# One-hots of the expert gate maps, token by token: pointer-scalar instructions in place of broadcast compares and products

## The chip, the cores and the metric

One Trainium2 chip, one of its cores. The metric is the device time of one execution in microseconds, median over runs of the same program.

## The reference, cut to what matters

Two transformer blocks over 256 tokens of width 1024 in f32. The first has a short convolution mixer, an attention mixer and two gated MLPs; the second a hybrid mixer and, last, the PEER feed-forward, where the change lies:

```python
def peer_ffn(x, w_q, sub_keys, u_tab, v_tab):      # 128 x 128 experts, 8 heads, 16 of them a head and token
...
    cand_idx = top_i[..., 0, :, None] * PEER_NKEYS + top_i[..., 1, None, :]
    best_s, pos = lax.top_k(cand, K)
    eidx = jnp.take_along_axis(cand_idx, pos, axis=-1)
    gate = jax.nn.softmax(best_s, axis=-1)
    hpre = jnp.einsum("nd,nhkd->nhk", xc, u_tab[eidx])
    act = gate * jax.nn.gelu(hpre, approximate=False)
    return jnp.einsum("nhk,nhkd->nd", act, v_tab[eidx])
```

Each token has 8 x 16 = 128 chosen experts. An expert has two keys, a (first sub-key) and b (second sub-key), each 0 to 127.

## The kernel before, in words

**Weights.** All weight matrices come as 546 chunks of 128 x 1024 f32 through a ring of three (`RING`), loaded by DMAs on SP's queue (L370). Each chunk is split in two fp32r halves: ACT writes the high half (`split_hi`, L383), then DVE and POOL write the rest, `raw - hi` (`split_lo`, L397), DVE the columns up to `cut` and POOL those behind it; in the expert stage the cut is 384, so DVE does 384 columns and POOL 640. TensorE multiplies a chunk with three products per 128 columns (L428, L429, L430), 24 matmuls a chunk. When it is done, ACT and then DVE and POOL take the chunk three places on.

**Expert stage.** The kernel gathers nothing. It goes through all 128 x 128 experts: 128 chunks upward (`UP0`, one for each key a, all keys b on the partitions) and 128 chunks downward (`DOWN0`). The gelu of the upward results lies in `emap` [b, a, token]. It is multiplied by a map of gates [b, a] for each token, which is zero where the token has not chosen the expert. A token's map is a matrix product over its 128 choices (on the partitions): `hot_b` (choice x 128, one where b is the choice's second key) times `hot_a` (choice x 64, the choice's gate where a is its first key). The gate is split in three bf16 parts so that bf16 matmuls keep its precision; hence three `hot_a` and three matmuls a token (L1495). 64 of the keys a make a half; eight tokens (`GT`) make a batch, 32 batches (`NB`) a half.

**The loops around the change.** `peer_dve` is DVE's program of the stage. In `second` (half 0, beside the second half of the upward chunks), a batch is: `hots`, two `walk_dve` (L397, 384 columns), `take_gates` of the batch before (L1485, `emap` times the map in PSUM). In `third` (half 1, beside the first half of the downward chunks) it is: `z_rest` (L1591, the low half of the gated experts), `hots`, `walk_dve`, `z_rest`, `walk_dve`, `take_gates`. `fourth` does the last 64 downward chunks and has no one-hots. TensorE's batch is two chunks (48 matmuls of 256 columns) and then `gates_of_batch_pe` (24 matmuls of 64 columns), which waits for `hot_ready`. `hots` in turn waits for `gm_done`, the gate matmuls of the batch before, as there is one set of `hot_a` and `hot_b`. Each engine runs its own instructions in the order written; there is no planner.

`hots` itself, for eight tokens at once: L1470 compares an iota with the first key, both inputs broadcast, into `hot_a[:, 2]` (512 columns); L1472 does the same for the second key into `hot_b` (1024 columns); then DVE waits for L1470's result (`dc.need`), and L1476 multiplies it with the three gate parts, the last in place, behind one more wait (`dc.link`).

`steps` writes the first rounds (up to `first`) and the last as straight code and the rest as a loop on the engine, six batches a turn here; in a loop, addresses and semaphore values that depend on the round are computed in registers by the engine's queue.

Of the kernel before, what the change touches and what calls it, by code (L numbers as in the profile page):

```python
# [16 lines left out]
ALU = mybir.AluOpType  # L17
# [3 lines left out]
P = 128  # L21
# [74 lines left out]
def steps(eng, chain, lo, hi, body, fn, first=0, per=0):  # L96

    n = lo
    while n < min(first, hi):
        fn(Step(n))  # L100
        n += 1
    turns = (hi - n) // body
    if turns > 1:
        with eng.Fori(0, turns) as i:
            if chain is not None:
                at = chain.n
                chain.i, chain.per = i, per * body
            for u in range(body):
                fn(Step(n + u, body, i))
            if chain is not None:  # L110
                assert chain.n - at == per * body, (chain.n - at, per, body)
                chain.n = at + per * body * turns
                chain.i = None
        n += body * turns
    while n < hi:
        fn(Step(n))
        n += 1
# [16 lines left out]
HALF = NKEY // 2  # L134
GT = 8


def build(nc, stream, xT, par, con, alibi_t, wg, wcmpk, wcmpv, peT, subk, y):
# [141 lines left out]
    idx = b_.take(2, T, dt=BF16)  # L280
    gate_left = b_.take(1, T)
    gate_part = b_.take(3, T, dt=BF16)
    iota_b = b_.take(P, dt=BF16)
    hot_b, hot_a = b_.take(GT, P, dt=BF16), b_.take(3, GT, HALF, dt=BF16)
# [120 lines left out]
    def walk_dve(dve, st, a, b):  # L405
        split_lo(dve, nc.vector, st, a, b + RING)
# [5 lines left out]
    def range_dve(dve, lo, hi):  # L412
        steps(dve, None, lo, hi, RING, lambda st: walk_dve(dve, st, 1, 0))
# [331 lines left out]
    def prev(st, n=1):  # L745
        return Step(st.s - n, st.stride, st.i)
# [714 lines left out]

    NB = T // GT

    def hots(dve, dc, half, st):
        if half or st.s >= 1:
            dve.wait_ge(gm_done, st.lin(1, NB * half))
        tok = bass.ds(st.lin(GT), GT)
        sa, sb_ = [P, GT, HALF], [P, GT, P]
        iota = iota_b
        dc.mark(nc.vector.tensor_tensor(hot_a[:, 2], iota[:, half * HALF:half * HALF + HALF].unsqueeze(1).broadcast_to(sa),  # L1470
                                        idx[:, 0, tok].unsqueeze(2).broadcast_to(sa), ALU.is_equal))
        nc.vector.tensor_tensor(hot_b, iota.unsqueeze(1).broadcast_to(sb_),  # L1472
                                idx[:, 1, tok].unsqueeze(2).broadcast_to(sb_), ALU.is_equal)
        dc.need()
        for i in range(3):
            ins = nc.vector.tensor_tensor(hot_a[:, i], hot_a[:, 2],  # L1476
                                          gate_part[:, i, tok].unsqueeze(2).broadcast_to(sa), ALU.mult)
            if i == 1:
                dc.link(ins)
        ins.then_inc(hot_ready, 1)  # L1480

    def take_gates(dve, half, st):
        dve.wait_ge(gm_done, st.lin(1, NB * half + 1))
        v = emap_of(half, st)
        nc.vector.tensor_tensor(v, v, ps[:, 6 + st.mod(2), :].rearrange("p (t a) -> p t a", t=GT), ALU.mult)\  # L1485
            .then_inc(gm_taken, 1)
# [75 lines left out]
    def peer_dve(dve, dc):  # L1562

        done, us = 0, 0.0
        for price in peer_top(dve, dc):
            us += price
            while done < HALF and us >= 1.8 * (done + 1):
                walk_dve(dve, Step(done), 1, UP0)
                done += 1
        range_dve(dve, UP0 + done, UP0 + HALF)  # L1570
        dve.wait_ge(tk_act, 10)
        dc.link(nc.vector.tensor_tensor(gate_left[:, 0], ps[:, 2, 0:T], gate_part[:, 0], ALU.subtract))
        dc.link(nc.vector.tensor_copy(gate_part[:, 1], gate_left[:, 0]))
        dc.link(nc.vector.tensor_tensor(gate_part[:, 2], gate_left[:, 0], gate_part[:, 1], ALU.subtract))

        def second(st):
            hots(dve, dc, 0, st)
            for u in range(2):
                walk_dve(dve, st, 2, UP0 + HALF + u - 1) if st.s or u else None
            if st.s >= 1:  # L1580
                take_gates(dve, 0, prev(st))

        steps(dve, dc, 0, NB, 6, second, first=1, per=2)
        walk_dve(dve, Step(NKEY - 1), 1, UP0)
        take_gates(dve, 0, Step(NB - 1))

        def z_rest(st, a, b):

            p = st.mod(2, a, b)
            dve.wait_ge(ez_hi, st.lin(a, b + 1))  # L1590
            nc.vector.tensor_tensor(ez[p][1], emap[:, st.lin(a, b), :], ez[p][0].bitcast(F32), ALU.subtract)\  # L1591
                .then_inc(z_ready, 1)

        z_rest(Step(0), 1, 0)

        def third(st, last=False):
            z_rest(st, 2, 1)
            hots(dve, dc, 1, st)
            if st.s >= 1:
                walk_dve(dve, st, 2, DOWN0 - 1)  # L1600
            if not last:
                z_rest(st, 2, 2)
            walk_dve(dve, st, 2, DOWN0)
            if st.s >= 1:
                take_gates(dve, 1, prev(st))

        steps(dve, dc, 0, NB - 1, 6, third, first=1, per=2)
        third(Step(NB - 1), last=True)
        take_gates(dve, 1, Step(NB - 1))

        def fourth(st):
            z_rest(st, 1, 0)
            walk_dve(dve, st, 1, DOWN0 - 1)

        steps(dve, None, HALF, NKEY - RING, 6, fourth)
        for n in range(NKEY - RING, NKEY):
            fourth(Step(n))
        dve.wait_ge(chunk_done, NCH)
# [4 lines left out]
    with nc.Block() as block:  # L1623
# [110 lines left out]
        def _(dve):  # L1734
# [35 lines left out]
            range_dve(dve, CH["pq"], UP0 - RING)  # L1770
            range_dve(dve, UP0 - RING, UP0)
            peer_dve(dve, dc)
            residual_dve(dve, dc)
            norm_dve(dve, dc, 7, "fin2")
# [147 lines left out]
```

## Time and profile before

| | us |
|---|---|
| median of three runs | 2238.18 |
| lowest and highest of them | 2234.65 and 2238.45 |
| profiled execution, first to last instruction | 2237.8 |
| busy in it: PE, DVE, ACT, POOL | 1986.2, 1614.8, 875.4, 884.5 |

The times of instructions below are of the one profiled execution; the profile gives its span (2237.8 us) and no other time of its own. PE is TensorE, DVE VectorE, ACT ScalarE, POOL GpSimd. "L1476" is line 1476 of the kernel; a line can be a helper's, as L397, which both DVE and POOL run. A row of the timeline has the start, the time taken, the engine, line, operation, what is written and read (m is SBUF, ps is PSUM), shapes and a count; in brackets the idle time before it and what ended that. Rows of one line that follow each other are merged into one with their count. Neighbours on DVE overlap in it by some 0.08 us, so prices are read from start to start where that can be done.

### The profile page before, as it was taken

How to read it: one execution, taken by the hardware profiler on the slowest of the kernel's cores; microseconds unless marked ns; L12 is line 12 of the kernel's file. 1: busy time of each engine (PE TensorE's matmuls, PEld its weight loads, DVE VectorE, ACT ScalarE, POOL GpSimd, SP SyncE). 2: the span in 40 equal slices, each digit the busy share in tenths (PEclk: the TensorE clock that was granted, in tenths of full speed). 3: DMA queues.
4: the chain of work that ended last, by engine and by line, in shares of the span. 5: the costliest groups of instructions: out<-in, count | busy, mean ns of one | idle time of the engine just before them, and what ended most of it. 6: DMA issues, size and time to landing. Idle time of an engine off the chain costs nothing.

```text
span 2237.8 us, 44421 instructions
## 1 busy us (share of the span) xinstructions
PE 1986.2 (89%) x15848; PEld 1919.1 (86%) x15848; DVE 1614.8 (72%) x2502; ACT 875.4 (39%) x1317; POOL 884.5 (40%) x584
## 2 busy tenths in 40 slices
PE   7979988998999699797898999898897888879897
PEld 7979988887999699787797999898887888878887
DVE  5568877545888423545655499779999999996665
ACT  4333433433434353633443455533333222324443
POOL 3524442303444153101254355654444333335553
PEclk9989998858999798657998999999999888889999
DMA  5535553404555153100264355543433333334443
GB/s 197 182 98 188 177 175 104 132 0 151 178 187 178 57 183 119 48 1 1 93 202 157 113 177 163 166 142 132 139 142 113 115 120 120 114 117 154 153 159 103
DMA packets 80278, 293.72 MB, mean 131 GB/s; under 512 B 8960, under 2 KB 9120, under 8 KB 79824
## 3 DMA queue, kind: packets, MB, share of 16 engines
q1 hardware_dynamic: 79632, 289.96, 38.9%
q0 software_dynamic: 576, 2.79, 0.3%
q8 instruction: 48, 0.79, 0.1%
q14 instruction: 22, 0.18, 0.0%
HBM read 291.67 MB, written 1.05 MB: 131 GB/s over the span
## 4 chain that ended last, share of the span: by engine, by line
PE 62%; DVE 23%; issue 9%; ACT 4%; DVEq 1%; DMA 0%; ACTq 0%; POOL 0%; SPq 0%; POOLq 0%
PE ps L428 17%; PE ps L430 16%; PE ps L429 16%; DVE m L1476 5%; DVE m L397 4%; DVE m L1591 3%; PE ps L434 3%; DVE m L1485 2%; PE ps L469 2%; DVE m L1470 2%; ACT m L383 1%; PE ps L759 1%; PE ps L758 1%; DVE m L521 1%; PE ps L1495 1%
## 5 line engine op out<-in xcount | busy, mean ns | idle before, releaser
L428 PE MATMUL ps<-m,m 128*128 128x256 f32 x4336 | 1270.9, 293 | 124.0 <-DVE m L1591 48.7
L397 POOL TENSOR_TENSOR m<-m,m 128x352 fp32r<-128x352 f32 (+1 forms) x546 | 867.4, 1590 | 1148.3 <-ACT m L383 1148.0
L429 PE MATMUL ps<-m,m 128*128 128x256 f32 x4336 | 1253.6, 289 | 0.0
L430 PE MATMUL ps<-m,m 128*128 128x256 f32 x4336 | 1251.3, 289 | 0.0
L428 PEld LDWEIGHTS ps<-m,m 128*128 128x128 f32 x4336 | 859.1, 198 | 140.0 <-issue 70.2
L429 PEld LDWEIGHTS ps<-m,m 128*128 128x128 f32 x4336 | 859.8, 198 | 0.6 <-issue 0.2
L430 PEld LDWEIGHTS ps<-m,m 128*128 128x128 f32 x4336 | 859.2, 198 | 0.0
L397 DVE TENSOR_TENSOR m<-m,m 128x672 fp32r<-128x672 f32 (+1 forms) x546 | 531.5, 985 | 407.2 <-ACT m L383 406.0
L383 ACT ACTIVATE m<-m 128x1024 fp32r<-128x1024 f32 x546 | 575.7, 1055 | 604.4 <-PE ps L430 586.1
L1476 DVE TENSOR_TENSOR m<-m,m 128x512 bf16<-128x512 bf16 x192 | 172.4, 923 | 9.6 <-DVE m L1476 1.5
L1591 DVE TENSOR_TENSOR m<-m,m 128x256 fp32r<-128x256 f32 x128 | 167.9, 1313 | 9.8 <-ACT m L1551 9.6
L1533 ACT ACTIVATE m<-ps 128x256 f32 (+1 forms) x128 | 49.2, 384 | 231.2 <-PE ps L430 231.1
L434 PEld LDWEIGHTS ps<-m,m 128*128 128x128 f32 (+1 forms) x412 | 75.5, 268 | 32.9 <-issue 16.6
L1495 PE MATMUL ps<-m,m 128*128 128x64 bf16 x1536 | 56.2, 194 | 47.5 <-DVE m L1476 47.5
L434 PE MATMUL ps<-m,m 128*128 128x128 f32 (+1 forms) x412 | 87.8, 380 | 11.5 <-ACT m L884 9.7
L1495 PEld LDWEIGHTS ps<-m,m 128*128 128x128 bf16 x1536 | 48.6, 98 | 55.4 <-DVE m L1476 37.5
L1485 DVE TENSOR_TENSOR m<-m,ps 128x512 f32 (+1 forms) x64 | 84.6, 1323 | 0.0
L1472 DVE TENSOR_TENSOR m<-m,m 128x1024 bf16<-128x1024 bf16 x64 | 77.6, 1212 | 0.0
L469 PE MATMUL ps<-m,m 128*128 128x256 f32 x128 | 45.1, 529 | 32.1 <-ACT m L500 32.1
L469 PEld LDWEIGHTS ps<-m,m 128*128 128x128 f32 x128 | 34.5, 277 | 41.2 <-ACT m L500 27.3
L594 ACT ACTIVATE m<-m 128x256 f32<-128x256 f32 x44 | 18.4, 418 | 126.5 <-DVE m L556 126.5
L813 ACT ACTIVATE m<-m,m 128x128 f32<-128x128 f32 x64 | 28.6, 447 | 84.5 <-PE ps L434 76.3
(200 smaller groups left out, 1292.4 us busy)
## 6 DMA issues: line engine op xcount, KB each, us to landing
m<-stream SPq DMA_DIRECT2D x546, 512.0 KB, 3.4
m<-alibi_t POOLq DMA_DIRECT2D x1, 1536.0 KB, 8.6
m<-con SPq DMA_DIRECT2D x1, 1353.0 KB, 10.2
m<-xT SPq DMA_DIRECT2D x1, 1024.0 KB, 4.9
y<-m SPq DMA_DIRECT2D x4, 256.0 KB, 2.4
m<-wcmpk POOLq DMA_DIRECT2D x1, 512.0 KB, 5.1
m<-wcmpv POOLq DMA_DIRECT2D x1, 512.0 KB, 5.7
m<-par SPq DMA_DIRECT2D x1, 178.0 KB, 5.3
```

What stands on the lines that cost most here:

```text
L383: nc.scalar.activation(w_hi[:, r, :], raw[:, r, :], ACT.Copy).then_inc(hi_done, 1)
L397: ops.tensor_tensor(w_lo[:, r, cols], raw[:, r, cols], w_hi[:, r, cols].bitcast(F32), ALU.subtract)\
L428: nc.tensor.matmul(out, lhs[0], rhs[0], start=start, stop=False, **kw)
L429: nc.tensor.matmul(out, lhs[0], rhs[1], start=False, stop=False, **kw)
L430: return nc.tensor.matmul(out, lhs[1], rhs[0], start=False, stop=stop, **kw)
L434: return nc.tensor.matmul(out, v, unit, start=True, stop=True)
L469: ins = nc.tensor.matmul(ps[:, 7, 0:T], ones[:, 0:P], sq[:, j, :], start=(j == 0), stop=(j == 7))
L1472: nc.vector.tensor_tensor(hot_b, iota.unsqueeze(1).broadcast_to(sb_), idx[:, 1, tok].unsqueeze(2).broadcast_to(sb_), ALU.is_equal)
L1476: ins = nc.vector.tensor_tensor(hot_a[:, i], hot_a[:, 2], gate_part[:, i, tok].unsqueeze(2).broadcast_to(sa), ALU.mult)
L1485: nc.vector.tensor_tensor(v, v, ps[:, 6 + st.mod(2), :].rearrange("p (t a) -> p t a", t=GT), ALU.mult)\
L1495: ins = nc.tensor.matmul(out, hot_b[:, q, :], hot_a[:, i, q, :], start=i == 0, stop=i == 2)
L1591: nc.vector.tensor_tensor(ez[p][1], emap[:, st.lin(a, b), :], ez[p][0].bitcast(F32), ALU.subtract)\
```

## The change

`hots` no longer works on eight tokens at once. For each of the eight tokens of a batch it issues four `tensor_scalar` instructions. The first compares the iota (128 columns) with the token's second key, a pointer scalar (one value a partition), and writes the token's part of `hot_b`. Three more compare 64 columns of the iota with the first key and multiply by one of the three gate parts, both pointer scalars, and write the token's part of `hot_a[:, i]`. No product reads a compare's result any more, so both waits of DVE on itself go, and with them the chain object `dc`. The two loops of batches on DVE become straight code (`first=NB`). TensorE's program and the semaphores between engines stay.

```diff
-    def hots(dve, dc, half, st):
+    def hots(dve, half, st):
         if half or st.s >= 1:
             dve.wait_ge(gm_done, st.lin(1, NB * half))
-        tok = bass.ds(st.lin(GT), GT)
-        sa, sb_ = [P, GT, HALF], [P, GT, P]
-        iota = iota_b
-        dc.mark(nc.vector.tensor_tensor(hot_a[:, 2], iota[:, half * HALF:half * HALF + HALF].unsqueeze(1).broadcast_to(sa),
-                                        idx[:, 0, tok].unsqueeze(2).broadcast_to(sa), ALU.is_equal))
-        nc.vector.tensor_tensor(hot_b, iota.unsqueeze(1).broadcast_to(sb_),
-                                idx[:, 1, tok].unsqueeze(2).broadcast_to(sb_), ALU.is_equal)
-        dc.need()
-        for i in range(3):
-            ins = nc.vector.tensor_tensor(hot_a[:, i], hot_a[:, 2],
-                                          gate_part[:, i, tok].unsqueeze(2).broadcast_to(sa), ALU.mult)
-            if i == 1:
-                dc.link(ins)
+        for q in range(GT):
+            one_tok = bass.ds(st.lin(GT, q), 1)
+            nc.vector.tensor_scalar(hot_b[:, q, :], iota_b, idx[:, 1, one_tok], None, ALU.is_equal)
+            for i in range(3):
+                ins = nc.vector.tensor_scalar(hot_a[:, i, q, :], iota_b[:, half * HALF:half * HALF + HALF],
+                                              idx[:, 0, one_tok], gate_part[:, i, one_tok],
+                                              ALU.is_equal, ALU.mult)
         ins.then_inc(hot_ready, 1)
...
-        steps(dve, dc, 0, NB, 6, second, first=1, per=2)
+        steps(dve, None, 0, NB, 6, second, first=NB)
...
-        steps(dve, dc, 0, NB - 1, 6, third, first=1, per=2)
+        steps(dve, None, 0, NB - 1, 6, third, first=NB)
```

(The two calls `hots(dve, dc, ...)` lose `dc` as well.)

## Rows read from the trace of the kernel before

**Rows 1.** The page: busy time by engine, and the group of L1476.
```profile
PE 1986.2 (89%) x15848; PEld 1919.1 (86%) x15848; DVE 1614.8 (72%) x2502; ACT 875.4 (39%) x1317; POOL 884.5 (40%) x584
...
L1476 DVE TENSOR_TENSOR m<-m,m 128x512 bf16<-128x512 bf16 x192 | 172.4, 923 | 9.6 <-DVE m L1476 1.5
```

**Rows 2.** Busy time by stretches: `second`, then `third`.
```profile
core 0: us, PE busy (x) PEld busy (x) DVE busy (x) ACT busy (x) POOL busy (x), PEclk, DMA share, GB/s
1469.00:1712.00 243.00, 214.52 (x2278) 208.82 (x2276) 235.95 (x253) 86.01 (x128) 112.85 (x64) 0.98 0.39 134
1712.00:2005.00 293.00, 241.56 (x2280) 235.98 (x2280) 279.43 (x319) 86.45 (x127) 111.55 (x63) 0.87 0.34 115
```

**Rows 3.** L1472 in each stretch: ns min/median/max, first and last start (us).
```profile
L1472 DVE TENSOR_TENSOR m<-m,m x32: 1207/1212/1226, 1469.1 to 1705.5; 128x1024 bf16<-128x1024 bf16 x32
...
L1472 DVE TENSOR_TENSOR m<-m,m x32: 1205/1212/1218, 1716.9 to 2000.9; 128x1024 bf16<-128x1024 bf16 x32
```

**Rows 4.** TensorE's timeline in `second`, and its waits there (us, times, longest).
```profile
1566.96 0.87 PE L1495 MATMUL ps<-m,m 128*128 128x64 bf16 x24 [0.89 <-DVE m L1476]
1567.87 0.28 PE L429 MATMUL ps<-m,m 128*128 128x256 f32 x1
...
1568.70 0.28 PE L430 MATMUL ps<-m,m 128*128 128x256 f32 x1
...
PE ps L1495 <- DVE m L1476: 19.2, 17, 2.1
```

**Rows 5.** DVE's timeline over one batch of `second`.
```profile
1581.81 1.01 DVE L397 TENSOR_TENSOR m<-m,m 128x384 fp32r<-128x384 f32 x2
1582.75 1.35 DVE L1485 TENSOR_TENSOR m<-m,ps 128x512 f32 x1
1584.02 0.80 DVE L1470 TENSOR_TENSOR m<-m,m 128x512 bf16<-128x512 bf16 x1
...
1587.91 2.39 DVE L397 TENSOR_TENSOR m<-m,m 128x384 fp32r<-128x384 f32 x2
```

**Rows 6.** POOL's timeline over the same batch.
```profile
1582.44 1.82 POOL L397 TENSOR_TENSOR m<-m,m 128x640 fp32r<-128x640 f32 x1 [1.10 <-ACT m L383]
1587.38 2.02 POOL L397 TENSOR_TENSOR m<-m,m 128x640 fp32r<-128x640 f32 x1 [3.11 <-ACT m L383]
```

**Rows 7.** L1591 over the span: ns min/median/max, first and last start.
```profile
L1591 DVE TENSOR_TENSOR m<-m,m x128: 403/1741/1799, 1715.6 to 2217.8; 128x256 fp32r<-128x256 f32 x128
```

**Rows 8.** The timeline near 1384 us, DVE and POOL: scalar instructions without pointer.
```profile
1383.87 0.30 DVE L1424 TENSOR_SCALAR m<-m 128x256 uint32<-128x256 uint32 x1
1384.08 1.66 DVE L1425 TENSOR_SCALAR m<-m 128x256 uint32<-128x256 uint32 x1
...
1383.94 1.65 POOL L397 TENSOR_TENSOR m<-m,m 128x640 fp32r<-128x640 f32 x1 [1.00 <-ACT m L383]
```

**Rows 9.** Two lines over the span: with a pointer scalar, and without.
```profile
L521 DVE SCALAR_TENSOR_TENSOR m<-m,m,m x64: 476/478/487, 15.4 to 2234.6; 128x256 f32<-128x256 f32 x64
...
L726 DVE TENSOR_TENSOR m<-m,m x16: 418/426/426, 358.6 to 408.1; 128x256 f32<-128x256 f32 x16
```

**Rows 10.** DVE's timeline at 446 us: 64 columns from PSUM, pointer scalar in SBUF.
```profile
446.53 0.28 DVE L944 TENSOR_SCALAR m<-ps,m 128x64 f32 x1 [0.16 <-DVE m L841]
446.73 0.28 DVE L945 TENSOR_SCALAR m<-ps,m 128x64 f32 x1
```

**Rows 11.** DVE's timeline at 1301 us: two instructions that start closest together.
```profile
1301.77 0.07 DVE L1401 MATCH_VALUE_LOAD m<-m,m 128x8 f32 x1
1301.83 0.28 DVE L1401 FIND_INDEX8 m<-m,m 128x8 uint32<-128x128 f32 x1
```

**Rows 12.** The timeline at 32 us, POOL and DVE: `tensor_scalar` from SBUF with pointer.
```profile
31.59 1.63 POOL L397 TENSOR_TENSOR m<-m,m 128x352 fp32r<-128x352 f32 x1 [1.26 <-ACT m L383]
...
32.77 0.59 DVE L553 TENSOR_SCALAR m<-m,m 128x256 f32<-128x256 f32 x1
```

**Rows 13.** Busy time by stretches, straight code of many small DVE instructions.
```profile
1280.00:1340.00 60.00, 58.14 (x485) 57.93 (x484) 58.91 (x244) 30.76 (x44) 33.94 (x20) 1.00 0.52 175
```

More of the change, by code:

```diff
@@ L1576, in second @@
         def second(st):
-            hots(dve, dc, 0, st)
+            hots(dve, 0, st)
             for u in range(2):
@@ L1597, in third @@
             z_rest(st, 2, 1)
-            hots(dve, dc, 1, st)
+            hots(dve, 1, st)
             if st.s >= 1:
```

## The prediction

> **What bounds the kernel now.** I read the page first: VectorE (DVE) is busy for 72% of the span and TensorE for 89%, so over the whole span TensorE looks like the limit, and the products of L1476 are the largest DVE group that the change touches [rows 1]. A mean over stages says little, so I cut the span with the view of busy time by stretches. From 1469 to 1712 us (up half of the expert stage: `second`, 32 batches of eight tokens) DVE is busy for 236 of 243 us, and from 1712 to 2005 us (`third`, 32 batches) for 279 of 293 us [rows 2]. Here DVE is the bound. The first and last starts of L1472, which runs once a batch, give the pace: (1705.5 - 1469.1) / 31 = 7.63 us a batch in `second`, (2000.9 - 1716.9) / 31 = 9.16 us in `third` [rows 3]. TensorE needs less: the 24 gate matmuls take up to 0.87 us, and the chunk matmuls come every (1568.70 - 1567.87) / 7 = 0.119 us, 48 a batch, 5.7 us, so some 6.5 us a batch at the full clock; it waits for L1476 [rows 4].
>
> The DVE timeline shows how a batch is spent [rows 5]. The one-hots (L1470, L1472, three of L1476) run from 1584.02 to 1587.91: **3.89 us**, nothing in their way. The two L397 at 1581.81 take 0.94 us, L1485 1.27 us. So a free batch is 3.89 + 0.94 + 1.27 = 6.10 us, and 7.63 - 6.10 = **1.53 us** is something else. The timeline of POOL names it [rows 6]: its subtraction starts at 1587.38 and ends at 1589.40, and the DVE pair of L397 that starts at 1587.91 takes 2.39 instead of 1.01 us. A DVE instruction on two SBUF inputs stands still until POOL's ends. POOL's other one, at 1582.44, lies mostly beside L1485, which reads PSUM, and costs little. POOL runs two a batch, some 1.6 us each without its own waiting: 3.2 us, of which DVE loses 1.53. In `third` two L1591 come on top, 0.40 us each when free [rows 7], less the 0.08 by which neighbours overlap in this view: free 6.10 + 0.64 = 6.74 us, the other 2.42 us blocked or idle.
>
> **The change, part by part.** Removed, a batch: five instructions of 0.6 to 1.2 us and two waits on DVE's own results, together the 3.89 us. Added: 32 `tensor_scalar`, eight with 128 columns and one pointer scalar, 24 with 64 columns and two. The loops become straight code; that drops register work which DVE's queue does beside running instructions, so I count it as nothing. No DMA, matmul or semaphore between engines moves: `hot_ready` still comes after the last write, so TensorE cannot start on the first token early.
>
> What does one cost? The trace has no such form in bf16 with two pointers, so I build it up. *Streaming.* L1472 (1024 columns, median 1212 ns [rows 3]) against L726 (256 columns, 426 ns [rows 9]) gives (1212 - 426) / 768 = 1.02 ns a column, one a cycle. L1424, a `tensor_scalar` from SBUF to SBUF without pointer [rows 8], does 256 columns in 0.30 us, 0.13 less than L726: two columns a cycle. I take that rate: 0.067 us for 128 columns, 0.033 for 64. *Fixed part.* L1424 starts 0.21 us before the next, less 0.13 of streaming is 0.08. A pointer is not free: L521 takes 478 ns where L726, the same columns without one, takes 426, so 0.052 us more [rows 9]: 0.13. A second way: L944 and L945, 64 columns with one pointer, start 0.20 us apart [rows 10]; 0.065 of it is streaming at one a cycle, 0.135 is fixed. They agree; I take **0.13 us**. *Second pointer.* No row; nothing to 0.055 us; I take nothing, as both come from the same place in one instruction. So 0.197 us for hot_b and 0.163 for each hot_a: a token 0.197 + 3 x 0.163 = 0.686, a batch 8 x 0.686 = **5.5 us** against 3.89. The break-even price is 3.89 / 32 = 0.122 us an instruction, and the columns hardly matter: the fixed part alone exceeds it.
>
> Bounds of the price: below, the closest starts on DVE, 0.06 us (MATCH_VALUE_LOAD, then the next) [rows 11], plus streaming: 8 x (0.127 + 3 x 0.093) = 3.25 us. Above, a full second pointer and one column a cycle: 8 x (0.263 + 3 x 0.252) = 8.2 us; with the second pointer but two columns a cycle 8 x (0.197 + 3 x 0.218) = 6.8 us.
>
> The Trainium skill (VectorE: DVE Perf Modes, the perf-mode tier table) lets a bf16 `tensor_scalar` from SBUF to SBUF stream four elements a cycle, and `tensor_tensor` two. By that the new ones would cost 4.8 us a batch in place of 5.5, and the time would be some 43 us below my forecast. No row here shows four a cycle; and L1472, a `tensor_tensor` broadcast along its columns, runs at one, not two [rows 3].
>
> *Blocking.* One might hope that one-source instructions escape POOL. They don't: L1425 starts at 1384.08 behind POOL's start at 1383.94 and takes 1.66 us where L1424 took 0.30 [rows 8], and L553, a `tensor_scalar` from SBUF with a pointer, takes 0.59 us, ending at 33.36, 0.14 us behind POOL's end at 33.22 [rows 12]. The Trainium skill (SBUF — State Buffer, SBUF: two separate sides) says the same of this port pair and gives it to whoever starts first for the whole instruction; by that rule, the trace agrees. With a longer stretch of blockable work, fewer POOL instructions fall beside L1485. In `second` I raise the loss from 1.53 to 2.1 us (`third`, whose batches are as long as the new ones, loses 2.42 with its idle time; 3.2 is the most); in `third` I leave 2.42.
>
> **Sum.** `second`: 0.94 + 1.27 + 5.5 + 2.1 = 9.8 us, +2.2 a batch, x 32 = +70. `third`: 6.74 - 3.89 + 5.5 + 2.42 = 10.8, +1.6, x 32 = +52. All else: 0, for no other stage runs this code, and ACT, POOL and the stream only follow TensorE. Together +122 us. The profiled execution spans 2237.8 us, 0.4 below the median of the three runs, 2238.18; forecast **2360 us**. Late next is TensorE: it would idle 3.3 us or more a batch in both stages. In `third`, where it idles now, the granted clock is 0.87 [rows 2]; I expect 0.75 to 0.9 in both. Even if half a batch's work ran at 1.2 GHz, its 6.5 us would be 9.8, no more than DVE's pace; if all did, 13.0 us, it would set it.
>
> **Rivals.**
> *Faster.* The pointer is fetched beside the instruction before, and short instructions follow each other at the 0.06 us of MATCH_VALUE_LOAD plus streaming: 3.25 us a batch, 0.64 less, x 64 = -41: 2197 us. It decides from 0.122 us an instruction downwards. For it: nothing in the trace shows short bf16 streams otherwise; against it: L944 at 64 columns still pays the whole fixed part [rows 10]. The Trainium skill (VectorE: DVE Perf Modes, The TRN2 errata) gives 58 cycles plus the columns by the mode's factor, 77 and 94 ns here, 2.6 us a batch; that would be some -80 us, TensorE's 6.5 us then being the floor in `second`. The same section warns that many small tiles pay the fixed cost each time. Chance 0.10 for either.
> *Second pointer priced like the first.* 6.8 us a batch, 1.3 more, x 64 = +85: 2445 us. Chance 0.18.
> *Clock.* TensorE idles so long that it stays at 1.2 GHz: 13.0 us a batch, against 9.8 and 10.8: 3.2 and 2.2 more, x 32 = +173 on the forecast: about 2530. Against it: 0.87 in `third` is a mix of the two levels, mostly 2.4 GHz, and at the low level TensorE would be busy all the time. Chance 0.03.
> *The straight code starves DVE.* Some 2,500 more instructions must be fetched. Against it: 244 DVE instructions in 60 us, straight code, kept it busy for 58.9 [rows 13]; the new pace is lower. Chance 0.02, and it only adds.
> *No difference*: the price happens to be 0.12 us. Chance 0.03; 2238.
> The forecast itself, price 0.14 to 0.19 us and a loss of 1.5 to 2.8 us a batch: 0.64.
>
> **How the numbers follow.** The range goes from the cheap end of the forecast (a fixed part of 0.11 us, so 4.9 us a batch, and a loss of 1.6 and 2.0: 8.7 and 9.8 us a batch, about 2290) to the second pointer with its spread (2450); outside lie the faster rival, the clock and a bit of each edge, 2 in 10. About 0.2% (4.5 us) is what a measurement of this kernel can tell from no change. Faster 0.11, within 0.03, slower 0.86.
>
> **What would show it.** In the profile after: the new instructions start 0.15 to 0.17 us (64 columns) and about 0.2 us (128) apart when POOL is idle; some of them last 1.6 to 1.8 us while POOL works; batches 9 to 11 us apart; TensorE's wait before the gate matmuls at 3 us a batch; the last stage unchanged at 220 us. It is wrong if the starts are under 0.12 us apart, or if the new ones run on while POOL works.

## The result, and the profile after

The changed kernel takes **2398.99 us** (2397.09 to 2401.06) against 2237.82 us for the kernel before, measured beside it: ratio 1.0727, 95% interval 1.0711 to 1.0742, slower by 161 us. The forecast was 2360 us, slower by 122, range 2290 to 2450.

Busy time by stretches of the kernel after, cut where `second` and `third` begin and end (columns as in [rows 2]):

```profile
core 0: us, PE busy (x) PEld busy (x) DVE busy (x) ACT busy (x) POOL busy (x), PEclk, DMA share, GB/s
1469.00:1805.00 336.00, 240.59 (x2281) 234.04 (x2279) 334.42 (x1121) 86.11 (x130) 108.32 (x64) 0.88 0.29 101
1805.00:2165.00 360.00, 256.82 (x2296) 250.42 (x2297) 359.11 (x1180) 85.64 (x125) 108.21 (x63) 0.82 0.25 90
2165.00:2397.00 232.00, 199.82 (x1564) 191.24 (x1561) 151.65 (x143) 89.42 (x132) 120.08 (x62) 0.97 0.42 143
```

Nearly everything lost lies in two stretches. `second` is 336 us long where it was 247 (to the first one-hot of `third`), `third` some 360 where it was 292: 157 of the 159 us by which the two profiled executions differ. The stage begins at 1468.5 us in the trace before and at 1468.7 in this one. DVE is busy for 334 of 336 and for 359 of 360 us: it was the bound and is so more than before. From the first one-hot instruction of the first batch to that of the last, over 31, a batch takes 10.43 us in `second` (7.63 before) and 11.34 us in `third` (9.16 before, same reading as [rows 3]).

The two new lines over the span, where L1470, L1472 and L1476 were: L1469 writes hot_b, L1471 writes hot_a (ns min/median/max, first and last start):

```profile
L1469 DVE TENSOR_SCALAR m<-m,m x512: 233/243/1647, 1468.7 to 2163.5; 128x128 bf16<-128x128 bf16 x171
...
L1471 DVE TENSOR_SCALAR m<-m,m,m x1536: 282/290/1712, 1468.9 to 2164.0; 128x64 bf16<-128x64 bf16 x192
```

The *smaller* instruction lasts longer, 290 ns for 64 columns against 243 for 128. It is the one with two pointers. DVE's timeline within a batch of `second` gives the starts:

```profile
1533.11 0.25 DVE L1469 TENSOR_SCALAR m<-m,m 128x128 bf16<-128x128 bf16 x1
1533.28 0.71 DVE L1471 TENSOR_SCALAR m<-m,m,m 128x64 bf16<-128x64 bf16 x3
1533.90 0.25 DVE L1469 TENSOR_SCALAR m<-m,m 128x128 bf16<-128x128 bf16 x1
1534.06 1.98 DVE L1471 TENSOR_SCALAR m<-m,m,m 128x64 bf16<-128x64 bf16 x3
1535.95 0.24 DVE L1469 TENSOR_SCALAR m<-m,m 128x128 bf16<-128x128 bf16 x1
1536.11 0.70 DVE L1471 TENSOR_SCALAR m<-m,m,m 128x64 bf16<-128x64 bf16 x3
1536.73 0.24 DVE L1469 TENSOR_SCALAR m<-m,m 128x128 bf16<-128x128 bf16 x1
1536.90 1.99 DVE L1471 TENSOR_SCALAR m<-m,m,m 128x64 bf16<-128x64 bf16 x3
```

and POOL's beside it, where [rows 6] stood:

```profile
1534.43 1.57 POOL L397 TENSOR_TENSOR m<-m,m 128x640 fp32r<-128x640 f32 x1 [3.47 <-ACT m L383]
1536.88 1.55 POOL L397 TENSOR_TENSOR m<-m,m 128x640 fp32r<-128x640 f32 x1 [0.89 <-ACT m L383]
```

A free token takes 1533.90 - 1533.11 = 0.79 us, a batch eight times that, 6.3 us. By the medians of start to start over all of them it is 0.163 us for hot_b and 0.206 for each hot_a, 0.781 a token, **6.25 us** a batch against 3.89. And two groups of three that should take 0.7 us take 2.0: each has one instruction that stands still through one of POOL's two, and ends 0.04 us behind it. TensorE waits for the one-hots before each batch's gate matmuls (L1489, L1495 in the kernel before), 194.4 us in all, 3.0 a batch:

```profile
PE ps L1489 <- DVE m L1471: 194.4, 62, 5.9
```

### The profile page after: what moved, and what is told of

It reads as the page before. It is cut to its first block, busy times and chain, and to the rows that moved or that the text cites. A ratio compares the mean times of both kernels' runs of the same rounds, so it can differ in the third digit from the quotient of the medians.

```text
span 2397.2 us, 45347 instructions
## 1 busy us (share of the span) xinstructions
PE 2029.8 (85%) x15848; PEld 1959.7 (82%) x15848; DVE 1790.2 (75%) x4230; ACT 874.4 (36%) x1317; POOL 876.2 (37%) x584
## 4 chain that ended last, share of the span: by engine, by line
PE 55%; DVE 38%; ACT 3%; issue 3%; DMA 0%; DVEq 0%; POOL 0%; SPq 0%; ACTq 0%; POOLq 0%
DVE m L1471 17%; PE ps L428 15%; PE ps L429 15%; PE ps L430 15%; DVE m L1469 5%; DVE m L397 3%; DVE m L1585 3%; DVE m L1479 3%; PE ps L434 3%; PE ps L469 2%; PE ps L759 1%; ACT m L383 1%; PE ps L758 1%; DVE m L521 1%; PE ps L777 1%
## 5 line engine op out<-in xcount | busy, mean ns | idle before, releaser
L397 POOL TENSOR_TENSOR m<-m,m 128x352 fp32r<-128x352 f32 (+1 forms) x546 | 859.2, 1575 | 1316.0 <-ACT m L383 1315.8
L428 PEld LDWEIGHTS ps<-m,m 128*128 128x128 f32 x4336 | 872.1, 201 | 107.4 <-issue 63.4
L429 PEld LDWEIGHTS ps<-m,m 128*128 128x128 f32 x4336 | 871.2, 201 | 0.6 <-issue 0.2
L430 PEld LDWEIGHTS ps<-m,m 128*128 128x128 f32 x4336 | 868.5, 200 | 0.0
L397 DVE TENSOR_TENSOR m<-m,m 128x672 fp32r<-128x672 f32 (+1 forms) x546 | 485.4, 900 | 408.1 <-ACT m L383 406.9
L1471 DVE TENSOR_SCALAR m<-m,m,m 128x64 bf16<-128x64 bf16 x1536 | 460.5, 356 | 0.0
L1489 PE MATMUL ps<-m,m 128*128 128x64 bf16 x1536 | 75.7, 219 | 194.4 <-DVE m L1471 194.4
L1489 PEld LDWEIGHTS ps<-m,m 128*128 128x128 bf16 x1536 | 66.8, 115 | 206.8 <-DVE m L1471 140.7
L1469 DVE TENSOR_SCALAR m<-m,m 128x128 bf16<-128x128 bf16 x512 | 157.5, 308 | 1.1 <-PE ps L1489 1.1
L1585 DVE TENSOR_TENSOR m<-m,m 128x256 fp32r<-128x256 f32 x128 | 141.1, 1104 | 2.0 <-ACT m L1545 2.0
L1479 DVE TENSOR_TENSOR m<-m,ps 128x512 f32<-128x512 f32 x64 | 82.7, 1294 | 0.0
L469 PEld LDWEIGHTS ps<-m,m 128*128 128x128 f32 x128 | 34.7, 278 | 41.2 <-ACT m L500 27.4
```

Source lines behind the costliest of these rows:

```text
L397: ops.tensor_tensor(w_lo[:, r, cols], raw[:, r, cols], w_hi[:, r, cols].bitcast(F32), ALU.subtract)\
L428: nc.tensor.matmul(out, lhs[0], rhs[0], start=start, stop=False, **kw)
L429: nc.tensor.matmul(out, lhs[0], rhs[1], start=False, stop=False, **kw)
L430: return nc.tensor.matmul(out, lhs[1], rhs[0], start=False, stop=stop, **kw)
L469: ins = nc.tensor.matmul(ps[:, 7, 0:T], ones[:, 0:P], sq[:, j, :], start=(j == 0), stop=(j == 7))
L1469: nc.vector.tensor_scalar(hot_b[:, q, :], iota_b, idx[:, 1, one_tok], None, ALU.is_equal)
```

## The experiments

Each was timed beside the kernel before. Line numbers shift with the edits, so the gate matmul is L1488, L1489, L1495, L1497 or L1498 in what follows. First, those that take the change apart.

**The straight code alone.** The kernel before with `first=NB` in both calls of `steps`:

```diff
-        steps(dve, dc, 0, NB, 6, second, first=1, per=2)
+        steps(dve, dc, 0, NB, 6, second, first=NB, per=2)
...
-        steps(dve, dc, 0, NB - 1, 6, third, first=1, per=2)
+        steps(dve, dc, 0, NB - 1, 6, third, first=NB, per=2)
```

> The kernel before with its two DVE loops of batches written as straight code, nothing else. My theory (the price of the small instructions makes the loss): no difference, 2238 us within 5, batches 7.6 and 9.2 us apart. Rival (straight code itself costs, through fetching or through the order of waits): at least a quarter of the 161 us, so 2278 us or more.

Measured: 2233.18 us, ratio 0.9984 (0.9973 to 0.9996), batches 7.53 and 9.15 us apart. The straight code costs nothing; it may give 4 us.

**The loops kept.** The other way round: the changed kernel with `first=1`.

```diff
-        steps(dve, None, 0, NB, 6, second, first=NB)
+        steps(dve, None, 0, NB, 6, second, first=1)
```

(and the same for `third`)

> The changed kernel with its two DVE loops of batches kept as loops (as in the kernel before), so that the addresses of keys and gates are computed by DVE's queue. In the kernel before, such register work comes 0.11 to 0.13 us apart in the queue. Queue theory: a 64-column instruction needs two of them, more than the 0.206 us that it takes itself, so starts 0.22 to 0.26 us apart, hots 7 us or more a batch, time 2440 us or more. Rival (the queue works ahead and hides it): 2399 us.

Measured: 2397.56 us, ratio 1.0732 (1.0708 to 1.0756), as the changed kernel; batches 10.43 and 11.34 us, starts 0.163 and 0.206 us. My theory of the queue was wrong and the rival right. The queue's rows for the line show why:

```profile
L1471 DVEq FUSED_REGOPS  x960: 57/67/82, 1480.0 to 2150.6; - x192
L1471 DVEq ALU_OP  x480: 40/40/40, 1480.1 to 2150.4; - x160
```

That is 1440 for the 1440 instructions in the loops (60 batches of 24): one each, not two. Where the queue works ahead (at 1480 us), a token's four, hot_b's among them, take 0.54 us from start to start, and the engine needs 0.781 us a token; so they run beside the instructions before them.

**One pointer less.** The product with the gate left out of hot_a (the result then lacks the gates):

```diff
-                                              idx[:, 0, one_tok], gate_part[:, i, one_tok],
-                                              ALU.is_equal, ALU.mult)
+                                              idx[:, 0, one_tok], None, ALU.is_equal)
```

> The changed kernel with hot_a written by a compare with one pointer scalar alone: the product with the gate is left out. In the changed kernel the 64-column instructions start 0.206 us apart, the 128-column ones 0.163. Pointer theory (every pointer scalar costs 0.05 to 0.06 us): 64 columns with one pointer start 0.15 us apart, hots take 8 x (0.163 + 3 x 0.15) = 4.9 us in place of 6.25, time 2399 - 64 x 1.35 = about 2313 us. Rival (a second pointer is free, 0.2 us is the least for 64 columns): starts stay at 0.2 us, time 2399 us.

**No pointer at all.** Constants in their places, both operations of hot_a kept (keys and gates are left out):

```diff
-            nc.vector.tensor_scalar(hot_b[:, q, :], iota_b, idx[:, 1, one_tok], None, ALU.is_equal)
+            nc.vector.tensor_scalar(hot_b[:, q, :], iota_b, 3.0, None, ALU.is_equal)
...
-                                              idx[:, 0, one_tok], gate_part[:, i, one_tok],
-                                              ALU.is_equal, ALU.mult)
+                                              3.0, 1.0, ALU.is_equal, ALU.mult)
```

> The changed kernel with constants in place of all pointer scalars; hot_a keeps its two operations, the keys and gates are left out of the one-hots. Pointer theory: fixed part 0.08 us, so 0.11 us for 128 columns and 0.095 for 64, hots 3.2 us a batch, batches some 6.9 and 8.2 us apart, time about 2190 us, below the kernel before. Rival (the second operation costs, not the second pointer): 64 columns still start 0.04 us further apart than 128 columns do, hots 4 us or more, time 2240 us or more.

Measured: 2304.09 us (ratio 1.0302, 1.0271 to 1.0334) and 2157.46 us (0.9653, 0.9631 to 0.9674). Hot_a with one pointer, hot_a with none, and hot_b with none:

```profile
L1471 DVE TENSOR_SCALAR m<-m,m x1536: 222/229/1631, 1468.1 to 2067.0; 128x64 bf16<-128x64 bf16 x192
```

```profile
L1471 DVE TENSOR_SCALAR m<-m x1536: 161/169/1591, 1470.5 to 1923.2; 128x64 bf16<-128x64 bf16 x192
...
L1469 DVE TENSOR_SCALAR m<-m x512: 175/182/1595, 1470.4 to 1923.0; 128x128 bf16<-128x128 bf16 x171
```

A ladder: 169, 229, 290 ns for none, one, two pointers. From start to start (medians): 0.086, 0.146, 0.206 us. **Each pointer costs 0.060 us, the second as much as the first.** e2_one_pointer takes the product away together with the pointer, so it can't tell the two apart; hot_b can. It has one operation, 128 columns, and starts 0.163 us before the next with its pointer and 0.102 without: 0.061 for a pointer alone. Take that off e2_one_pointer's 0.146 and 64 columns with one operation and no pointer would be 0.085, with two operations they measure 0.086: the second operation costs nothing. Between 128 and 64 columns lie 0.016 us (0.102 and 0.086; 0.163 and 0.146 with a pointer), 0.25 ns a column, a quarter of the 1.02 ns that the prediction found for one column a cycle: four a cycle. So the price is 0.069 + 0.060 a pointer + 0.00026 a column. Without pointers the small instructions beat the broadcast form: the changed form was lost on its scalars, not on its number. The whole times say less than the starts do, since something else ends a batch as the one-hots get shorter: batches of e3_no_pointer are 6.71 us apart in `second`, 0.2 above TensorE's 6.5, and it came out 33 us below the 2190 expected.

**Only hot_b by token.** e1_straight with the one line:

```diff
-        nc.vector.tensor_tensor(hot_b, iota.unsqueeze(1).broadcast_to(sb_),
-                                idx[:, 1, tok].unsqueeze(2).broadcast_to(sb_), ALU.is_equal)
+        for q in range(GT):
+            one_tok = bass.ds(st.lin(GT, q), 1)
+            nc.vector.tensor_scalar(hot_b[:, q, :], iota, idx[:, 1, one_tok], None, ALU.is_equal)
```

> The kernel before in straight code, with hot_b alone written by eight pointer-scalar compares a batch; hot_a stays with its broadcast compare and three products. Theory of the price by instruction: 8 x 0.163 = 1.30 us in place of 1.135, 0.17 a batch, 64 batches: 11 us over e1_straight (2233), so 2244. The other 150 us of the loss belong to the 24 hot_a instructions. Rival (splitting into small instructions itself disturbs the stage, whatever its sum): 2260 us or more.

Measured: 2238.62 us, ratio 1.0010 (0.9995 to 1.0024), 5 us over e1_straight, where 11 were expected. Little or nothing of the 161 us is hot_b's; the hot_a instructions, 24 of the 32, have it. The compares for hot_b start 0.163 us apart here too.

**POOL out of the way.** The split's border in the expert stage moved, in the changed kernel and in the kernel before:

```diff
-CUT, CUT_PEER = 672, 384
+CUT, CUT_PEER = 672, 1016
```

> The changed kernel with the split of the expert stage's chunks nearly all on DVE: 1016 columns, POOL has 8. DVE's L397 grows by 0.66 us a chunk, 1.3 a batch. Lock theory (POOL's instruction holds the one-source DVE instructions up, 1.7 us a batch in second and 1.9 in third): no one-hot instruction lasts over 0.5 us, batches 8.46 + 1.3 = 9.8 us in second (10.16 now) and 9.1 + 1.3 = 10.4 in third (11.0 now); the first half of the upward chunks, where DVE picks the top 16, gets slower. Rival (the long instructions have another cause): long ones stay, batches 11.5 and 12.3 us.

> The kernel before, its one-hots untouched, with 1016 of the 1024 columns of the expert chunks' split on DVE and 8 on POOL (the same edit as in e4_pool_out). Lock theory: free batches of 6.1 + 1.3 = 7.4 us in second (7.6 now) and 6.7 + 1.3 = 8.0 in third (9.2 now), and the last stage 20 us shorter as in e4_pool_out, so 2238 - 7 - 37 - 20 = about 2174 us. Rival (in the kernel before POOL's help is worth its waits, since broadcast tensor_tensor hides them): 2238 us or slower.

Measured: 2322.57 us (1.0388, 1.0371 to 1.0405), batches 9.67 and 10.37 us; and 2168.23 us (0.9691, 0.9676 to 0.9706), batches 7.22 and 8.00 us. The one-hots in the first, with POOL left 8 columns:

```profile
L1471 DVE TENSOR_SCALAR m<-m,m,m x1536: 282/290/346, 1469.0 to 2109.2; 128x64 bf16<-128x64 bf16 x192
...
L1469 DVE TENSOR_SCALAR m<-m,m x512: 232/243/287, 1468.8 to 2108.6; 128x128 bf16<-128x128 bf16 x171
```

The longest is 346 ns, where it was 1712. DVE does 2.6 times the columns of the split and both kernels gain, 76 and 69 us: POOL's help cost DVE more in waits than it took off. The gain isn't all in the stretches of the change. In e5_pool_out_before `second` is 13 us shorter and `third` 36, and what comes after the last one-hots 22; in e4_pool_out it is 24, 30 and 22. (The stage itself begins between 1463.8 and 1471.0 us in these profiles, whatever was changed in it, so a few us of a profiled execution are not the edit's.) Of what I expected, one part failed: the upward half before `second` did not get slower (`second` starts at 1468.8 us in e4_pool_out). In the second kernel L397 takes 1208 ns for 1016 columns, L1476 lasts 690 ns in the mean, not 923, and L1591 lasts 424 in the median, not 1741 [rows 7]:

```profile
L397 DVE TENSOR_TENSOR m<-m,m 128x1016 fp32r<-128x1016 f32 x128 | 152.0, 1208 | 0.4 <-ACT m L383 0.4
L1476 DVE TENSOR_TENSOR m<-m,m 128x512 bf16<-128x512 bf16 x192 | 127.0, 690 | 9.6 <-DVE m L1476 1.5
...
L1591 DVE TENSOR_TENSOR m<-m,m x128: 401/424/453, 1697.7 to 2142.3; 128x256 fp32r<-128x256 f32 x128
```

**A better way to the same aim.** The broadcast form runs at one column a cycle [rows 3]. If that comes from the inputs that repeat along the innermost dimension, a layout with tokens innermost would double it: the key and the gate then have step one, and the iota is stored repeated, once. The price: TensorE reads its one-hots with a step. First with all eight tokens innermost, a step of 16 bytes, for hot_a, then for hot_b too:

```diff
...
+    iota_t = nc.alloc_sbuf_tensor_at("iota_t", [P, P * GT], BF16, offset=base + 4 * (A0 + NKEY * T))[:, :]\
+        .rearrange("p (k t) -> p k t", k=P)
...
-        dc.mark(nc.vector.tensor_tensor(hot_a[:, 2], iota[:, half * HALF:half * HALF + HALF].unsqueeze(1).broadcast_to(sa),
-                                        idx[:, 0, tok].unsqueeze(2).broadcast_to(sa), ALU.is_equal))
+        dc.mark(nc.vector.tensor_tensor(hot_a[:, 2], iota_t[:, half * HALF:half * HALF + HALF, :],
+                                        idx[:, 0, tok].unsqueeze(1).broadcast_to(sa), ALU.is_equal))
...
-                ins = nc.tensor.matmul(out, hot_b[:, q, :], hot_a[:, i, q, :], start=i == 0, stop=i == 2)
+                ins = nc.tensor.matmul(out, hot_b[:, q, :], hot_a[:, i, :, q], start=i == 0, stop=i == 2)
```

> The kernel before with hot_a laid out with the token innermost, so that no tensor_tensor input is broadcast along its innermost dimension (an iota repeated eight times is made once, 0.5 us per partition row); TensorE then reads its 64 moving columns with a step of eight. Theory (the broadcast along the columns keeps these tensor_tensor at one column a cycle, and with the token innermost they run at two): L1470 and L1476 take 0.34 us in place of 0.60, hots 1.07 us less a batch; second comes near TensorE's floor of 6.5 us, time about 2238 - 32 x 0.9 - 32 x 1.0 = 2175 us. Rival (they stay at one a cycle, or the stepped reads slow the gate matmuls by as much): 2238 us or more.

> As e7_token_inner_a, with hot_b token innermost too, so that the stationary operand is read with a step of eight. Theory: another 0.53 us a batch off DVE; second is at TensorE's floor, third gains: about 2155 us. Rival (the stepped weight load is slow: 24 of them a batch, 0.1 us each now, so a doubling gives 2.4 us a batch back): 2230 us or more.

Measured: 2257.68 us (1.0099, 1.0085 to 1.0114) and 2320.60 us (1.0383, 1.0362 to 1.0403): the rivals' side. DVE did as the theory said, and TensorE paid. The compare, the gate matmul and its load in e7_token_inner_a:

```profile
L1471 DVE TENSOR_TENSOR m<-iota_t,m x64: 409/426/451, 1471.0 to 2022.0; 128x512 bf16<-128x512 bf16 x64
...
L1497 PEld LDWEIGHTS ps<-m,m x1536: 95/117/128, 1475.1 to 2029.9; 128*128 128x128 bf16 x192
L1497 PE MATMUL ps<-m,m x1536: 273/294/296, 1475.1 to 2030.0; 128*128 128x64 bf16 x192
```

The compare takes 426 ns where L1470 took about 682 when free; the one-hots take 2.7 us when free. But the gate matmul takes 294 ns where it took 193, and from start to start it is 0.116 us where it was 0.029. Batches of `second` are 8.51 us apart with 5.7 of chunks in them, and DVE now waits for the gate matmuls (L1497, 77.9 us). With the stationary operand stepped too, a batch takes 9.65 us. Of these 1.14 us more, only some 0.15 is the stepped operand itself: the gate matmuls start 0.122 us apart, 24 of them. So the time is on the rival's side, but not by the 2.4 us a batch of slower loads that it stood for. The rest is the clock in the chunk matmuls, granted at 0.88 in `second` where e7_token_inner_a had 0.99, though TensorE was busy for 307 of 310 us:

```profile
1469.00:1779.00 310.00, 307.36 (x2271) 305.54 (x2269) 142.40 (x255) 84.57 (x128) 112.51 (x64) 0.88 0.33 108
...
1600.20 0.28 PE L431 MATMUL ps<-m,m 128*128 128x256 f32 x1
...
1601.10 0.41 PE L430 MATMUL ps<-m,m 128*128 128x256 f32 x1
1601.31 0.41 PE L431 MATMUL ps<-m,m 128*128 128x256 f32 x1
```

In 23 of the 32 batches the clock is at its lower level (1.2 GHz) for some 3.4 us, and the chunk matmuls then come 0.213 us apart in place of 0.119; over the 48 of a batch that is 1.0 us in the mean. It falls 0.3 to 0.7 us behind the last of the gate matmuls. What makes it fall there and not in e7_token_inner_a is not shown.

Then in pairs of tokens, [pair, column, 2], a step of 4 bytes, alone and with the border of the split moved to 1016 and to 704:

```diff
...
+        sa, sb_ = [P, GT // 2, HALF, 2], [P, GT // 2, P, 2]
+
+        def of_pair(v, shape):
+            return v.rearrange("p (g t) -> p g t", t=2).unsqueeze(2).broadcast_to(shape)
+
+        dc.mark(nc.vector.tensor_tensor(hot_a[:, 2], iota_t[:, half * HALF:half * HALF + HALF, :].unsqueeze(1).broadcast_to(sa),
+                                        of_pair(idx[:, 0, tok], sa), ALU.is_equal))
+        nc.vector.tensor_tensor(hot_b, iota_t.unsqueeze(1).broadcast_to(sb_), of_pair(idx[:, 1, tok], sb_), ALU.is_equal)
...
+                ins = nc.tensor.matmul(out, hot_b[:, q // 2, :, q % 2], hot_a[:, i, q // 2, :, q % 2], start=i == 0, stop=i == 2)
```

> The kernel before with the one-hots laid out in pairs of tokens (pair, column, token of the pair): no tensor_tensor input is broadcast along its innermost dimension, and TensorE reads with a step of two bf16 (4 bytes) in place of the 16 of e7 and e8. Theory (two columns a cycle need only an innermost pair, and a step of 4 bytes is free for TensorE where 16 was not): hots 2.1 us a batch in place of 3.66, second at TensorE's floor of 6.5 to 6.7 us, third 7.5, so 2238 - 32 - 52 = about 2155 us. Rival (any step slows the gate matmuls): 2200 us or more.

> e12_pairs with 1016 of the split's columns on DVE and 8 on POOL. DVE in second 2.1 + 2.3 + 1.3 = 5.7 us a batch and 6.4 in third, without waits for POOL: both stages at TensorE's 6.5 to 6.7 us, and the last stage 20 us shorter as in e5: 2238 - 32 - 80 - 20 = about 2106 us. Rival (POOL's share is worth more once DVE has slack): 2155 us or more.

> e12_pairs with 704 columns on DVE and 320 on POOL, between the two: POOL's instruction is half as long (0.8 us in place of 1.6), so DVE waits less for each. Lock theory: a time between e12 and e13, about 2125 us. Rival (any instruction of POOL costs about as much as a long one): no better than e12.

Measured: 2132.77 us (0.9549, 0.9529 to 0.9569), **2099.08 us** (0.9391, 0.9370 to 0.9411) and 2106.09 us (0.9422, 0.9402 to 0.9442). The order is the one forecast for the lock, not the sizes: 2155, 2106 and 2125 us were expected, so the pairs alone gave 22 us more than that, and e14_pairs_cut704 lies close to e13_pairs_pool_out, not halfway. The last two are 7 us apart with intervals that overlap. The gate matmuls in e12_pairs are as short as in the kernel before, and so is the compare on DVE as in e7:

```profile
L1475 DVE TENSOR_TENSOR m<-iota_t,m x64: 408/422/429, 1468.0 to 1891.8; 128x512 bf16<-128x512 bf16 x64
...
L1498 PEld LDWEIGHTS ps<-m,m x1536: 96/97/103, 1470.9 to 1896.0; 128*128 128x128 bf16 x192
L1498 PE MATMUL ps<-m,m x1536: 191/193/205, 1470.9 to 1896.0; 128*128 128x64 bf16 x192
```

In e13_pairs_pool_out both stretches have changed their bound:

```profile
1469.00:1681.00 212.00, 208.36 (x2287) 206.85 (x2285) 180.91 (x259) 86.03 (x130) 65.92 (x64) 1.00 0.46 159
1681.00:1892.00 211.00, 210.11 (x2304) 208.73 (x2304) 200.64 (x319) 86.04 (x126) 19.57 (x63) 0.99 0.46 156
```

TensorE is busy for 208 of 212 and 210 of 211 us, at the full clock; the batches are 6.50 and 6.60 us apart, which is the 6.5 us that the prediction worked out as its floor [rows 4]. The pairs alone had brought `second` there already, and `third` nearly (e12_pairs: 6.49 and 6.85 us). Of the 34 us that POOL's columns add, the profiles have 8 in `third` and 23 in the last stage. This kernel beats the kernel before by some 136 us and the changed one by 300.

## Why the prediction was right, and which term was mis-sized

The time fell inside the range, and the direction, the bound and the waits for POOL were right. The price of an instruction, on which all rests, was wrong twice, in opposite directions; that the errors partly cancelled is luck.

**The bound.** Right: DVE set the pace in `second` and `third`, and 157 of the 159 us are there. The last stage stayed (230 and 232 us), and so did everything up to 1468 us.

**The price of an instruction.** The step that failed in size is "*Second pointer* ... I take nothing, as both come from the same place in one instruction": e2_one_pointer and e3_no_pointer show 0.060 us for it, a little over the value that I had kept as the upper end (0.055). The fixed part with one pointer, 0.13 us from two unrelated pairs of rows, was measured as 0.069 + 0.060 = 0.129. The streaming was half of what I took, four columns a cycle. By the Trainium skill (VectorE: DVE Perf Modes, the perf-mode tier table) it had to be four; by that rule, the trace agrees (0.25 ns a column). A token came to 0.781 us: 0.686 less 0.033 (hot_b's streaming) less 0.05 (hot_a's) plus 3 x 0.060. That is 6.25 us in place of 5.5 a batch, 0.75 x 64 = 48 us more; the second pointer alone would have been 92, and the faster streaming gave 43 back. Both signs that I gave for the starts failed: 0.206 us for 64 columns, not 0.15 to 0.17, and 0.163 for 128, not 0.2. And the mean price, 6.25 / 32 = 0.195 us, lies above the 0.14 to 0.19 to which I gave 0.64.

**The waits for POOL.** Right in kind and nearly in size. Free batches are 0.94 + 1.27 + 6.25 = 8.46 us and 6.74 - 3.89 + 6.25 = 9.10 us; the paces leave 1.97 and 2.24 us, where I had put 2.1 and 2.42: 0.13 and 0.18 less, some 10 us in all. So 122 + 48 - 10 = 160, measured 161. That these are waits for POOL, e4_pool_out shows: with 1.3 us more of L397 a batch and no waits it would be 9.8 and 10.4 us a batch, and it measures 9.67 and 10.37. One reading was off: the 3.89 us had something in their way. POOL's instruction of 1582.44 ends at 1584.26, L1470 starts at 1584.02 and takes 0.80 us in place of 0.68 [rows 5, 6]; with POOL out of the way the old one-hots take 3.78 (e5_pool_out_before, median). Put right, it moves the forecast by 4 us, in `third`.

**The rivals.** The second pointer priced like the first was one of them, with 0.18; its mechanism is what happened, so the forecast came within its range by a mechanism that it had given to a rival. The rival's 2445 us are too high, since it left the streaming at two a cycle. With both corrections (0.129 + 0.033 and 0.189 + 0.017 us) its own sum gives 6.24 us a batch and 2407, 8 above the measured time, as it keeps waits that were put some 10 us too high. The rival on the faster side fell: e3_no_pointer shows that its 0.093 us for 64 columns is nearly the price *without* pointers (0.086), so the pointer is not fetched beside the instruction before. The formula that the prediction took from the Trainium skill (VectorE: DVE Perf Modes, The TRN2 errata) gives 77 ns for 64 columns; it has no term for pointers, and the runs have 86 ns without them and 206 with two. Starving by straight code: e1_straight and e9_loops exclude it.

**The clock.** Granted 0.88 and 0.82 where I expected 0.75 to 0.9. It did not set the pace: TensorE was busy for 241 of 336 us, and waited for hot_a 3.0 us before each batch's gates, as forecast. In e8_token_inner_ab it does cost time.

**"L1472 runs at one [column a cycle], broadcast along its columns"** was right, but I made nothing of it; e12_pairs shows that 103 us lay in it.

## What to carry to other kernels

Price a small instruction by its fixed part and its pointer scalars first, and count both pointers: at 64 columns, 0.19 of 0.206 us had nothing to do with columns. Where a broadcast `tensor_tensor` in bf16 runs at one column a cycle, try a layout in which the innermost dimension of every input has step one, if only a pair long, before replacing it by many small instructions; and look at what the new step does to the engine that reads the result. Where two engines block each other, giving more work to the one that is the bound can still make it faster.

## What the runs showed of the hardware that was not expected

- A pointer scalar on DVE costs 0.060 us from start to start, the second as much as the first, also for 64 columns (bf16, e2_one_pointer and e3_no_pointer); a second operation costs nothing.
- TensorE reads bf16 operands with a step of 4 bytes as fast as packed ones (193 ns), with a step of 16 bytes not (294 ns, some 2.8 us a batch for 24 of them in place of 0.8). A stepped stationary operand adds to its load, 146 ns in e8_token_inner_ab against 117 in e7_token_inner_a, but only 0.006 us to the time from one gate matmul to the next:

```profile
L1495 PEld LDWEIGHTS ps<-m,m x1536: 142/146/172, 1471.8 to 2085.8; 128*128 128x128 bf16 x192
L1495 PE MATMUL ps<-m,m x1536: 293/302/324, 1471.8 to 2085.9; 128*128 128x64 bf16 x192
```

  The Trainium skill (SBUF — State Buffer, Door 1: The DMA port swizzle) has SBUF lines of 16 bytes that need two hits each for full speed; by that rule, the trace agrees: one hit a line at a step of 16 bytes, four at a step of 4. In the same place the Trainium skill counts a stride of 8 bf16, which is 16 bytes, as free; the runs say that it is not (0.116 us from start to start in place of 0.029). What a step of 8 bytes costs was not tried.
- In a kernel whose DVE was busy for 97% of `second` and 95% of `third`, moving 632 more columns a chunk onto it took 49 us off these two and 69 off the whole (e5_pool_out_before), for POOL's 640 columns held it up for longer. Whether some border between 704 and 1016 is better still was not tried.
- TensorE's granted clock can fall although the engine is busy all the time: 0.88 over `second` of e8_token_inner_ab, busy for 307 of 310 us. Why is open.
